# Six-layer float32 block: the start's loads, the companion unit, the index scores and the sparse heads put in another order

## The chip, the core and the metric

The kernel runs on one core of a Trainium2 chip. The metric is the time of the whole execution on the device, in microseconds (us). Engines: PE does matmuls, DVE and POOL elementwise work, ACT activations, SP issues most DMAs. Each engine takes its own queue in order; they meet at semaphores.

## The reference, cut to what matters

Sequence 256, model width 1024, batch 1. Six layers follow each other: a gated short convolution (A0), sparse attention (B0), latent attention (C0), a convolution again (A1), pooling (P0) and stick-breaking attention (S0), each as `x = x + mixer(rmsnorm(x))`. The change is in the first two.

```python
def short_conv_mixer(xn, w_in, conv_w, conv_b, w_out):
    bg, cg, hv, z = jnp.split(xn @ w_in, 4, axis=-1)
    u = cg * hv
    y = causal_depthwise_conv3(u, conv_w) + conv_b
    return (bg * y * jax.nn.silu(z)) @ w_out

def dsa_mixer(xn, positions, w_in, q_norm, k_norm, w_out):
    q, k, v, z, qi, ki, wi = jnp.split(xn @ w_in, cuts, axis=-1)   # 16 heads of 64; 8 index heads
    q = rope(rmsnorm(q, q_norm), positions)
    k = rope(rmsnorm(k, k_norm), positions)
    # qi and ki get a partial rope; per query block of 128:
    rel = jax.nn.relu(jnp.einsum("qhd,sd->qhs", qi_b, ki_b))
    score = jnp.einsum("qh,qhs->qs", w_b, rel)                      # masked by chunks of 64
    top_val, top_idx = lax.top_k(score, 64)
    # per head: softmax over the 64 chosen keys, times v
    return (o * jax.nn.silu(z)) @ w_out
```

## The kernel before

Weights are cut into **units**, 78 in all (A0 begins at 0, B0 at 10, C0 at 22, A1 at 36). A unit's weights land in a slot `raw` of 2 MB, ACT rounds it to `whi` (L409, or L417 in quarters), DVE subtracts to `wlo` (L779, L788), and PE runs three matmuls (xh·whi, xl·whi, xh·wlo) for each pair of tiles, so the product keeps float32's accuracy. There are two slots, so a unit's split runs one or two units ahead of PE. Each engine's order is written out by hand.

**Start.** SP issues the identity, x, the constants `cst`, `a_norm`, then unit 0 in eight pieces, the small parameters, then unit 1. PE transposes x, DVE copies it out and makes xh, xl. Meanwhile POOL works out the rope angles. It waits at its first instruction for the positions and for `cst`:

```python
pool.wait_ge(sem("pos_in"), 48)
pool.wait_ge(sem("cst_in"), 16)
```

and ACT, after the splits of units 0 and 1, waits for POOL's four `angle_ready` steps (L1368 writes the last) before it takes their sines (L496). Only behind that in ACT's queue stand the first unit's copy (L467) and the split of unit 2.

**Layer B** has twelve units. B0 is the index queries; B0+1 (72 columns) is the companion: the index key `ki` and the weights `wi`; B0+2 to B0+6 are q and k by tokens (512 columns); B0+7 k's last part; B0+8 and B0+9 v's rest and z; B0+10, B0+11 the output matrix. Token units are turned to channel-major by PE transposes (`turn_tokens(e)`, e = 0 to 4), after ACT copies them out (`token_raw`), DVE and POOL apply norm and rope (POOL's L1424 the norm factor), and ACT copies the turned result back (`token_out`). With the index queries and key turned, PE does eight index heads, ACT relu (L574), DVE sums them, and DVE picks the top 64 of each query block (`top64`). For each of 16 heads PE then computes scores (2 matmuls), DVE adds the choice and finds the row maximum (L1098, L1102), ACT takes the exponential (L621, L623), DVE divides (L1107, L1109), PE transposes p (L1798), ACT copies it (L630), and PE multiplies with v (PV). Between these, PE has one filler: a quarter of units B0+7, B0+8, B0+9, up to head 11. The silu of z is done on ACT at heads 4 and 12 (L606, with a table load to each side). The output units follow the last head as one block (`out_pair`).

Of the kernel before, what the change touches and what calls it, by code (L numbers as in the profile page):

```python
# [21 lines left out]
F32 = mybir.dt.float32  # L22
# [3 lines left out]
ALU = mybir.AluOpType  # L26
# [84 lines left out]
def build(nc, a, out):  # L111

    ctx = ExitStack()
    with ctx:
# [32 lines left out]
        pl = at("pl", [P, 4, T], F32R, arena_at + 35 * tile_bytes)  # L147
        upad = at("upad", [P, T + 2], F32, arena_at + 18 * tile_bytes)
# [8 lines left out]
        kis = at("kis", [P, NT, P], F32, arena_at + 42 * tile_bytes)  # L157
        ki_b = at("ki_b", [P, NT, 32], F32, arena_at + 43 * tile_bytes)
# [135 lines left out]
        def _(sp):  # L294
# [22 lines left out]
            def conv_layer(u0, j):  # L317

                src = a["a_w_in"][j].rearrange("(k p) (s c) -> s p k c", p=P, s=4)

                def step(b, f, guard):
# [17 lines left out]
                with sp.Fori(1, 4) as i:  # L339
                    for b in range(2):  # L340
                        step(b, i * 2 + b, i * 4 + 2 * (u0 + b) - 2)
# [3 lines left out]
            def small_inputs(first):  # L345

                rows = ((G_A, "a_norm", 16), (G_CW, "a_conv_w", 48), (G_CB, "a_conv_b", 16), (G_B, "b_norm", 8),
                        (G_C, "c_norm", 8), (G_N2, "norm_g_2", 16), (G_NF, "norm_f_2", 8),
                        (G_QL, "c_q_lat_norm", 3), (G_KVL, "c_kv_lat_norm", 2))
                for col, name, c in rows[:1] if first else rows[1:]:  # L350
                    sp.dma_start(grow[col:col + c, 0, :], a[name].rearrange("(n c) -> n c", c=P))\
                        .then_inc(sem("a_norm_in" if first else "grow_in"), 16)
                if first:
                    return
                others = [(grow[G_CQ:G_CQ + 1, 0, 0:96], a["c_q_norm"]), (grow[0:1, 1, 0:96], a["c_k_norm"]),
                           (grow[17:18, 1, 0:64], a["c_k_norm"][:, 0:64]),
                           (grow[1:17, 1, :], a["pool_scale_2"].rearrange("(n c) -> n c", c=P))]
                for dst, src in others:
                    sp.dma_start(dst, src).then_inc(sem("grow_in"), 16)
            sp.dma_start(ident, a["constants"][:, C_ID:C_ID + P]).then_inc(sem("ident_in"), 16)  # L360
            for t in range(NT):
                sp.dma_start(xrow[:, t, :], a["x"][0, t * P:(t + 1) * P, :]).then_inc(sem("x_in"), 16)
            sp.dma_start(cst[:, P:C_COLS], a["constants"][:, P:C_COLS]).then_inc(sem("cst_in"), 16)
            sp.wait_ge(sem("grow_clear"), 1)
            small_inputs(True)
# [38 lines left out]
        def _(act):  # L404
# [3 lines left out]
            def split_half(b, lo, hi):  # L408
                A(whi[b][:, lo:hi], raw[b][:, lo:hi], ACT.Copy).then_inc(hi_ready, 1)  # L409

            def split_quarter(u, q):

                if q == 0:
                    act.wait_ge(landed[u % 2], 64 * (u // 2 + 1))
# [6 lines left out]
            def split(u, part=(0, 1)):  # L421

                cut, end = half_cut(u)
                if 0 in part:
                    act.wait_ge(landed[u % 2], 64 * (u // 2 + 1))
# [6 lines left out]
            def renorm(m, gain):  # L432

                if gain is not None:
                    for n in range(NK):
# [3 lines left out]
                        if m == 0 and n == 3:  # L439
                            act.wait_ge(sem("first_half"), 64)  # L440
                            split_half(0, 0, half_cut(0)[0])
                if m == 0:
# [1593 lines left out]
```

## Time and profile before

| | us |
|---|---|
| median of 3 runs | 1081.18 |
| lowest, highest | 1076.1, 1084.76 |
| profiled execution | 1085.21 |
| its span | 1083.4 |
| PE busy | 1013.5 |
| DVE busy | 649.3 |
| ACT busy | 498.0 |
| POOL busy | 337.4 |

The profiled execution is one of its own; its span is what the profile covers, and 1.81 us of its time lie around the span. PE is busy 94% of the span, so what moves the time is a stretch in which PE waits, or runs at the lower clock, or is given more or less work.

### The profile page before, as it was taken

Reading aid. Unit: us, or ns where it says so; the run is one execution under the profiler, and the core shown is the slowest. Engines: PE = TensorE matmul, PEld = TensorE weight load, DVE = VectorE, ACT = ScalarE, POOL = GpSimd, SP = SyncE. Lnnn points to the kernel's source line nnn. Section 1 sums busy time; section 2 is a strip of 40 time slices with the busy share of each in tenths; the row PEclk is TensorE's granted clock in tenths of the full one; section 3 lists DMA queues with packets and bytes.
Section 4 is the critical chain, followed back from the end, with each engine's and each line's share of the span. In section 5 each row is a group of like instructions: output and inputs, shape, how many; then the busy total and the mean of one; then the engine's idle time right before and its main releaser. Section 6 shows DMA issues by size and latency. Waiting matters only on the chain.

```text
span 1083.4 us, 17563 instructions
## 1 busy us (share of the span) xinstructions
PE 1013.5 (94%) x7165; PEld 935.1 (86%) x7165; DVE 649.3 (60%) x998; ACT 498.0 (46%) x666; POOL 337.4 (31%) x270
## 2 busy tenths in 40 slices
PE   4799999899989989988999999899999999999798
PEld 4799998687759989755899999899999997988698
DVE  3477756895674554458457766677655644555632
ACT  3444345446663434427354336324444336474621
POOL 7944212441110310532143333776400200132400
PEclk8999998899979999759999999999999999999998
DMA  8668445322333313423067754434664462424400
GB/s 230 152 156 232 155 148 175 129 105 78 125 109 103 98 50 97 173 61 79 6 170 184 204 174 172 160 122 164 218 235 158 169 214 92 155 79 155 156 1 39
DMA packets 127526, 148.49 MB, mean 137 GB/s; under 512 B 12595, under 2 KB 83520, under 8 KB 127456
## 3 DMA queue, kind: packets, MB, share of 16 engines
q1 hardware_dynamic: 127008, 146.39, 42.1%
q0 software_dynamic: 448, 1.12, 0.4%
q8 instruction: 50, 0.82, 0.3%
q14 instruction: 20, 0.16, 0.0%
HBM read 146.44 MB, written 1.05 MB: 136 GB/s over the span
## 4 chain that ended last, share of the span: by engine, by line
PE 62%; DVE 8%; ACT 5%; POOL 3%; issue 3%; DVEq 0%; ACTq 0%; POOLq 0%
PE acc L1501 38%; PE aux L1501 23%; POOL arena L1374 1%; DVE wlo L779 1%; POOL arena L1375 1%; POOL arena L1373 1%; PE aux L1798 1%; ACT whi L417 1%; ACT arena L447 1%; DVE wlo L788 1%; DVE score L1056 1%; DVE work L1098 1%; DVE top L1055 1%; DVE sqy L989 0%; DVE arena L871 0%
## 5 line engine op out<-in xcount | busy, mean ns | idle before, releaser
L779 DVE TENSOR_TENSOR wlo<-raw,whi 128x2048 fp32r<-128x2048 f32 (+4 forms) x132 | 295.2, 2264 | 145.4 <-ACT whi L409 143.6
L1501 PE MATMUL acc<-xh,whi 128*128 128x256 f32 (+1 forms) x1200 | 346.0, 288 | 12.3 <-DVE wlo L779 10.1
L1501 PE MATMUL acc<-xl,whi 128*128 128x256 f32 (+1 forms) x1200 | 342.8, 286 | 0.0
L1501 PE MATMUL acc<-xh,wlo 128*128 128x256 f32 (+1 forms) x1200 | 342.7, 286 | 0.0
L409 ACT ACTIVATE whi<-raw 128x2048 fp32r<-128x2048 f32 (+4 forms) x132 | 215.1, 1661 | 118.1 <-PE aux L1501 66.5
L1501 PEld LDWEIGHTS acc<-xh,whi 128*128 128x128 f32 (+1 forms) x1200 | 233.3, 194 | 16.5 <-DVE wlo L779 10.4
L1501 PEld LDWEIGHTS acc<-xl,whi 128*128 128x128 f32 (+1 forms) x1200 | 233.6, 195 | 0.0
L1501 PEld LDWEIGHTS acc<-xh,wlo 128*128 128x128 f32 (+1 forms) x1200 | 233.4, 194 | 0.0
L1501 PE MATMUL aux<-yh,whi 128*128 128x256 f32 x384 | 108.9, 284 | 0.0
L1501 PE MATMUL aux<-yh,wlo 128*128 128x256 f32 x384 | 108.7, 283 | 0.0
L1501 PE MATMUL aux<-yl,whi 128*128 128x256 f32 x384 | 108.7, 283 | 0.0
L1445 POOL CAST yh<-ytmp 128x256 fp32r<-128x256 f32 x24 | 19.7, 822 | 232.5 <-DVE ytmp L1293 129.3
L1501 PE MATMUL acc<-whi,xh 128*128 128x512 f32 (+1 forms) x192 | 76.6, 399 | 3.6 <-DVE arena L871 1.5
L1501 PE MATMUL acc<-wlo,xh 128*128 128x512 f32 (+1 forms) x192 | 74.9, 390 | 0.0
L1501 PE MATMUL acc<-whi,xl 128*128 128x512 f32 (+1 forms) x192 | 74.8, 390 | 0.0
L1501 PEld LDWEIGHTS aux<-yh,whi 128*128 128x128 f32 x384 | 73.7, 192 | 0.3 <-issue 0.3
L1501 PEld LDWEIGHTS aux<-yl,whi 128*128 128x128 f32 x384 | 73.7, 192 | 0.0
L1501 PEld LDWEIGHTS aux<-yh,wlo 128*128 128x128 f32 x384 | 73.7, 192 | 0.0
L788 DVE TENSOR_TENSOR wlo<-raw,whi 128x1024 fp32r<-128x1024 f32 x48 | 58.4, 1218 | 0.4 <-ACT whi L417 0.3
L1501 PE MATMUL aux<-arena 64*128 64x128 f32 (+2 forms) x224 | 55.2, 382 | 2.5 <-ACT relu L574 1.6
L1373 POOL TENSOR_TENSOR arena<-arena 128x1024 f32<-128x1024 f32 x5 | 12.0, 2409 | 137.5 <-ACT arena L447 137.5
L417 ACT ACTIVATE whi<-raw 128x1024 fp32r<-128x1024 f32 x48 | 50.1, 1045 | 0.0
(283 smaller groups left out, 1724.8 us busy)
## 6 DMA issues: line engine op xcount, KB each, us to landing
raw<-in_a_w_in SPq DMA_DIRECT2D x60, 512.0 KB, 6.5
raw<-in_sb_w_in SPq DMA_DIRECT2D x48, 512.0 KB, 5.7
raw<-in_b_w_in SPq DMA_DIRECT2D x36, 512.0 KB, 5.2
raw<-in_pool_w_in SPq DMA_DIRECT2D x32, 512.0 KB, 5.8
raw<-in_a_w_out SPq DMA_DIRECT2D x16, 512.0 KB, 4.8
raw<-in_pool_w_out SPq DMA_DIRECT2D x16, 512.0 KB, 4.9
raw<-in_sb_w_out SPq DMA_DIRECT2D x16, 512.0 KB, 5.2
raw<-in_c_w_in SPq DMA_DIRECT2D x12, 512.0 KB, 5.4
```

The costliest lines, as they stand in the source:

```text
L409: A(whi[b][:, lo:hi], raw[b][:, lo:hi], ACT.Copy).then_inc(hi_ready, 1)
L417: ins = A(whi[u % 2][:, c * q:c * q + c], raw[u % 2][:, c * q:c * q + c], ACT.Copy)
L447: A(arena[:, 4 * n:4 * n + 4, :], xT[:, 4 * n:4 * n + 4, :], ACT.Square)\
L779: TT(wlo[b][:, lo:hi], raw[b][:, lo:hi], whi[b][:, lo:hi].bitcast(F32), ALU.subtract)\
L788: ins = TT(wlo[u % 2][:, c], raw[u % 2][:, c], whi[u % 2][:, c].bitcast(F32), ALU.subtract)
L1055: me.link(V.max(top8[:, :], s))
L1056: me.link(V.match_replace(s, top8[:, :], s, TAKEN))
L1098: ins = V.tensor_tensor_reduce(L[:, lo:hi], S[:, lo:hi], bias[:, lo:hi], -1.0, 3.0e38, ALU.add, ALU.min, st[:, n:n + 1])
L1373: me.link(TT(arena[:, 0:4, :], arena[:, 0:4, :], arena[:, 4:8, :], ALU.add))
L1374: me.link(TT(arena[:, 0:2, :], arena[:, 0:2, :], arena[:, 2:4, :], ALU.add))
L1445: nc.gpsimd.tensor_copy(hi, ytmp[:, :]).then_inc(sem("yh_ready"), 1)
L1501: return nc.tensor.matmul(out_, lhsT, rhs, start=start, stop=stop, skip_group_check=True)
```

## The change

Four things are changed.

1. **Loads at the start.** x comes in column halves. Unit 0's and unit 1's weights come in eight pieces by rows of the matrix. The constants are issued behind unit 0's eight pieces. Unit 2 has a buffer of its own (`raw_third`). The 13 small parameters go by ACT's queue. Units 0 and 1 are split in quarters, and layer A0's sum of squares goes ahead of unit 1's split on DVE.
2. **Companion.** B0+1 is computed channel-major (72 rows by 256), 24 matmuls in place of 48; ACT copies it to `kif`, and two transposes inside unit B0+2 give its token rows.
3. **Index scores.** One index head stands before each of the eight steps of unit B0+4, q's unit, in place of all eight behind B0+3. The turns of tokens are moved into the units (k = 2, 4 or 6), and the splits of B0+5 into the loop of relus.
4. **Sparse heads by pairs.** Both heads' scores are issued together, with two fillers for each pair, the pair's transposes one pair later, and its two PVs together behind the second filler. Half of output unit B0+10 is done as fillers 13 to 16; the other half and B0+11 follow.

```diff
                 if u0 == 0:
-                    dst = slot(0, 8, 512)
-                    for k, signal in ((0, sem("first_half")), (4, landed[0])):
-                        for s in range(4):
-                            sp.dma_start(dst[:, k:k + 4, s * P:s * P + P], src[s][:, k:k + 4, 0:P]).then_inc(signal, 16)
-                    small_inputs(False)
-                    step(1, 1, None)
+                    for k in range(8):
+                        first_tile(0, k).then_inc(sem(f"first_in{k // 2}"), 16)
+                    sp.dma_start(cst[:, P:C_COLS], a["constants"][:, P:C_COLS]).then_inc(sem("cst_in"), 16)
+                    for k in range(8):
+                        first_tile(1, k).then_inc(sem(f"second_in{k // 2}"), 16)
+                    whole(raw_third, 2, landed[0])
+                    step(1, 3, 4)
...
-            token_unit(B0 + 1, spread_at(1, 6))
+            unit(B0 + 1, [(acc[0:72, 2, 0:T], 0, 72)], xh, xl)
...
             taken("tok_raw", 2)
-            token_unit(B0 + 2)
...
+            token_unit(B0 + 2, ki_rows)
             taken("ki_raw", 2)
-            token_unit(B0 + 3)
-            taken("ki_out", 1)
-            taken("tok_out", 2)
-            for h in range(8):
...
+            token_unit(B0 + 3, ki_turn)
             taken("tok_raw", 4)
-            token_unit(B0 + 4)
-            turn_tokens(2)
+            token_unit(B0 + 4, index_scores)
             taken("tok_raw", 6)
-            token_unit(B0 + 5)
-            turn_tokens(3)
+            token_unit(B0 + 5, turn_at({2: 1}))
             taken("tok_raw", 8)
-            token_unit(B0 + 6)
+            token_unit(B0 + 6, turn_at({2: 2, 6: 3}))
...
+            def sparse_heads(q, k, v):
+
+                for j in range(HEADS // 2 + 1):
+                    if j < HEADS // 2:
+                        if j:
+                            pe.wait_ge(sem("logits"), 2 * j)
...
+                        for c, e in ((0, P), (P, T)):
+                            for i in (2 * j, 2 * j + 1):
...
+                    sparse_filler(2 * j)
+                    if j == 0:
+                        taken("v_ready", 2)
+                        turn_tokens(4)
+                    if j:
+                        for h in (2 * j - 2, 2 * j - 1):
+                            pe.wait_ge(sem("p_ready"), h + 1)
...
+                            ins.then_inc(sem("pt_psum"), 1)
+                    sparse_filler(2 * j + 1)
+                    if j:
+                        t = j - 1
+                        pe.wait_ge(sem("pt_ready"), 2 * t + 2)
+                        if t:
+                            pe.wait_ge(sem("y_ready"), 8 + t)
...
-            softmax_heads(0, pair(0), pair(8), vB)
-            out_pair(B0 + 10, 8)
+            sparse_heads(pair(0), pair(8), vB)
+            sparse_last_out()
```

POOL's program is the same in both kernels, and so are ACT's and DVE's loops over the 16 heads.

SP's queue from its first DMA, before (`raw_49` is unit 0's slot):

```order
L360 DMA cst<-in_constants 128x128
L362 DMA xrow<-in_x 128x1024 x2
L363 DMA cst<-in_constants 128x623
L351 DMA grow<-in_a_norm 16x128
L333 DMA raw_49<-in_a_w_in 128x4x128 x8
L351 DMA grow<-in_a_conv_w 48x128
L351 DMA grow<-in_a_conv_b 16x128
L351 DMA grow<-in_b_norm 8x128
```

and after the change:

```order
L360 DMA cst<-in_constants 128x128
L364 DMA xrow<-in_x 128x512 x4
L327 DMA raw_49<-in_a_w_in 128x4x128 x8
L346 DMA cst<-in_constants 128x623
L327 DMA raw_50<-in_a_w_in 128x4x128 x8
L333 DMA raw_third<-in_a_w_in 128x8x128 x4
L340 DMA raw_50<-in_a_w_in 128x8x128 x4
```

The constants (128x623) moved from the third place to behind unit 0's eight pieces, and the small parameters (`grow`) left this queue.

PE at the end of unit B0+3 and the first index scores, before (`aux<-arena` are the scores, `acc<-` the weights' matmuls):

```order
L1501 MATMUL acc<-whi_52,xh 128x512
L1501 MATMUL acc<-wlo_54,xh 128x512
L1501 MATMUL acc<-whi_52,xl 128x512
L1501 MATMUL aux<-arena 128x128
L1501 MATMUL aux<-arena 128x256
```

and after, the end of B0+3 and the first step of B0+4:

```order
L1549 MATMUL acc<-whi_52,xl 128x512
L1549 MATMUL aux<-arena 128x128
L1549 MATMUL aux<-arena 128x256
L1549 MATMUL acc<-whi_51,xh 128x512
L1549 MATMUL acc<-wlo_53,xh 128x512
L1549 MATMUL acc<-whi_51,xl 128x512
```

Before, seven more such pairs of scores follow at once; now six matmuls of 512 columns stand behind each pair (the first three are shown), and the next pair behind them.

PE within the heads, before, from the last filler matmuls of one head to the next head's (`aux<-cst,work` are the transposes of p, `acc<-work,vB` is PV, `aux<-arena` are scores):

```order
L1501 MATMUL acc<-xh,wlo_54 128x256
L1798 MATMUL aux<-cst,work 128x128 x3
L1501 MATMUL acc<-work,vB 64x256
L1501 MATMUL acc<-work,vB 64x128
L1501 MATMUL aux<-arena 128x128
L1501 MATMUL aux<-arena 128x256
L1501 MATMUL acc<-whi_51,xh 128x512
```

and after, at the same place:

```order
L1549 MATMUL acc<-xh,wlo_54 128x256
L1549 MATMUL acc<-work,vB 64x256 x2
L1549 MATMUL acc<-work,vB 64x128 x2
L1549 MATMUL aux<-arena 128x128 x2
L1549 MATMUL aux<-arena 128x256 x2
L1549 MATMUL acc<-whi_51,xh 128x512
```

PV and scores of two heads stand together; the six transposes of a pair stand between its two fillers, ahead of this piece.

## Rows read from the trace of the kernel before

**Rows 1.** The page: busy us, share of the span and instructions of each engine.

```profile
PE 1013.5 (94%) x7165; PEld 935.1 (86%) x7165; DVE 649.3 (60%) x998; ACT 498.0 (46%) x666; POOL 337.4 (31%) x270
```

**Rows 2.** The timeline of SP's queue: start, length of the issue in us.

```profile
2.13 0.43 SPq L363 DMA_DIRECT2D cst<-in_constants  x1
```

**Rows 3.** Tile views in that stretch: landing of `cst` (two transfers), then of `raw`'s first eight.

```profile
DMA to landing us min/median/max: 1.9/4.7/7.5
L333 SPq DMA_DIRECT2D raw<-in_a_w_in x8: 825/862/3312, 3.5 to 12.4; - x8
DMA to landing us min/median/max: 5.3/7.8/8.1
```

**Rows 4.** Timeline of POOL's angle chain, and the DVE split beside it.

```profile
9.91 0.40 POOL L1351 CAST arena<-table 128x256 f32<-128x256 int32 x1 [5.27 <-DMA pos_i<-in_positions]
...
22.42 2.15 POOL L1364 TENSOR_TENSOR work<-work,ang 128x96 f32<-128x96 f32 x1
25.19 0.39 POOL L1364 TENSOR_TENSOR work<-work,ang 128x96 f32<-128x96 f32 x1
...
22.03 2.29 DVE L779 TENSOR_TENSOR wlo<-raw,whi 128x2048 fp32r<-128x2048 f32 x1 [1.16 <-ACT whi L409]
...
48.87 1.07 POOL L1368 TENSOR_SCALAR work<-work 128x256 f32<-128x256 f32 x1
```

**Rows 5.** Timeline behind it, on ACT, DVE and PE: unit 2's first half.

```profile
49.97 0.72 ACT L496 ACTIVATE table<-work 128x256 f32<-128x256 f32 x2 [9.17 <-POOL work L1368]
...
50.86 1.91 ACT L409 ACTIVATE whi<-raw 128x2048 fp32r<-128x2048 f32 x1
...
55.15 0.39 PE L1501 MATMUL acc<-xh,whi 128*128 128x256 f32 x1 [3.08 <-DVE wlo L779]
```

**Rows 6.** Windows: busy us (instructions) on each engine, granted clock, DMA share, GB/s.

```profile
60.00:140.00 80.00, 80.00 (x669) 80.00 (x668) 56.18 (x66) 35.45 (x38) 28.35 (x22) 1.00 0.64 188
220.00:230.00 10.00, 10.00 (x50) 8.28 (x49) 9.86 (x15) 2.91 (x4) 7.50 (x4) 1.00 0.21 60
```

**Rows 7.** PE's timeline, the first index scores (four records for a head).

```profile
192.71 0.93 PE L1501 MATMUL aux<-arena 64*128 64x128 f32 x8
```

**Rows 8.** PE's timeline over one head of the sparse softmax.

```profile
267.07 0.86 PE L1501 MATMUL acc<-work,vB 128*64 128x256 f32 x4
267.86 0.92 PE L1501 MATMUL aux<-arena 64*128 64x128 f32 x4
268.71 0.50 PE L1501 MATMUL acc<-whi,xh 128*128 128x512 f32 x1
...
271.59 0.49 PE L1798 MATMUL aux<-cst,work 128*128 128x128 f32 x3
```

**Rows 9.** PE's timeline, first row of unit B0+1 and of B0+2.

```profile
160.15 0.28 PE L1501 MATMUL acc<-whi,xh 128*128 128x72 f32 x1
...
167.80 0.77 PE L1501 MATMUL acc<-whi,xh 128*128 128x512 f32 x1 [0.61 <-DVE wlo L779]
```

**Rows 10.** Timeline on DVE, POOL and PE where the heads begin.

```profile
245.51 0.28 DVE L1098 CUSTOM_DVE_ANT_0 work<-aux,pick 128x128 f32<-128x128 f32 x1
...
249.48 1.17 POOL L1424 TENSOR_TENSOR sqy<-sqy,hf 128x512 f32<-128x512 f32 x1
...
251.59 0.63 PE L1656 MATMUL acc<-cst,sqy 128*128 128x128 f32 x4 [2.36 <-ACT arena L544]
```

**Rows 11.** Timeline over head 12: ACT's silu between its table loads, and PE.

```profile
309.25 1.28 ACT L606 ACT_TABLE_LOAD   x1
310.54 1.06 ACT L606 ACTIVATE arena<-arena 128x1024 f32<-128x1024 f32 x1
...
312.25 1.08 PE L1501 MATMUL acc<-work,vB 128*64 128x256 f32 x2 [3.81 <-DVE ytmp L1078]
```

**Rows 12.** Windows over the heads, columns as in Rows 6.

```profile
252.00:310.00 58.00, 54.50 (x319) 42.58 (x316) 32.95 (x107) 34.54 (x73) 4.55 (x8) 0.97 0.20 73
310.00:320.00 10.00, 7.75 (x23) 4.37 (x23) 7.04 (x25) 7.85 (x15) 2.25 (x4) 0.58 0.38 122
```

More of the change, by code:

```diff
@@ L338, in conv_layer @@
                         step(b, b, 2 * (u0 + b) - 2)
-                with sp.Fori(1, 4) as i:
+                with sp.Fori(2 if u0 == 0 else 1, 4) as i:
                     for b in range(2):
@@ L343, in conv_layer @@
                     plain(u0 + 8 + h, a["a_w_out"][j], 4 * h, 0)
[L345 to L359, printed above, removed]
-            sp.dma_start(ident, a["constants"][:, C_ID:C_ID + P]).then_inc(sem("ident_in"), 16)
[L361 to L365, printed above, removed]
+            sp.dma_start(ident, a["constants"][:, C_ID:C_ID + P]).then_inc(sem("ident_in"), 16)
+            for half in range(2):
+                c = slice(512 * half, 512 * half + 512)
+                for t in range(NT):
+                    sp.dma_start(xrow[:, t, c], a["x"][0, t * P:(t + 1) * P, c]).then_inc(sem(f"x_in{half}"), 16)
             conv_layer(A0, 0)
@@ L424, in split @@
                 if 0 in part:
[L425 removed]
+                    act.wait_ge(landed[u % 2], 64 * (u // 2))
                     if u >= 2:
@@ L487, in _ @@
             renorm(0, G_A)
-            split(1)
+            for q in range(4):
+                first_quarter(1, q)
             root(0)
@@ L828, in renorm @@
                                 .then_inc(sem("xg_ready"), 1)
-                    if m == 0 and c in (2, 4):
-                        split(0, (c // 4,))
+                    if m == 0 and c:
+                        first_quarter(0, c - 1)
             def token_squares(m):
@@ L880, in _ @@
             renorm(0, G_A)
-            split(1)
             token_squares(0)
+            for q in range(4):
+                first_quarter(1, q)
             dve.wait_ge(sem("g_psum"), 1)
@@ L924, in _ @@
             split(B0 + 1)
-            factor(1)
+            factor(1, spread=False)
             split(B0 + 2, (0,))
@@ L1766, in v_unit, with sparse_filler @@
                     ins.then_inc(unit_done, 1)
+            def sparse_filler(f):
+                part = (2 * (f % 4), 2)
+                if f == 0:
+                    taken("tok_raw", 10)
+                if f == 4:
+                    taken("z_raw", 1)
+                if f == 8:
+                    taken("v_ready", 4)
+                if f < 12:
+                    if f // 4 == 1:
+                        v_unit(B0 + 8, 1, *part)
+                    else:
+                        unit(B0 + 7 + f // 4, in_tiles(1), xh, xl, part=part)
+                if 13 <= f < 17:
+                    if f == 13:
+                        taken("z_raw", 2)
+                    sparse_out(f - 13, 0)
@@ new lines, in sparse_out @@
+            def sparse_out(k, half):
+                wh, wl = w_view(B0 + 10, 4, 1024)
+                if k % 2 == 0:
+                    pe.wait_ge(lo_ready, 2 * (B0 + 10) + 1 + k // 2)
+                pe.wait_ge(sem("yl_ready"), 8 + k + 1)
+                for n in range(4):
+                    c = slice(512 * half + P * n, 512 * half + P * n + P)
+                    ins = three(sparse_out_tile(4 * half + n), wh[:, k, c], wl[:, k, c], yh[:, k, :], yl[:, k, :],
+                                k == 0 and n % 2 == 0)
+                if k == 3 and half == 1:
+                    ins.then_inc(unit_done, 1)
@@ new lines, in sparse_last_out @@
+            def sparse_last_out():
+                for k in range(4):
+                    sparse_out(k, 1)
+                u = B0 + 11
+                wh, wl = w_view(u, 4, 1024)
+                pe.wait_ge(lo_ready, 2 * u + 2)
+                pe.wait_ge(sem("yl_ready"), 16)
+                for n in range(NK):
+                    c = slice(P * n, P * n + P)
+                    for k in range(4):
+                        ins = three(sparse_out_tile(n), wh[:, k, c], wl[:, k, c], yh[:, 4 + k, :], yl[:, 4 + k, :], False)
+                    if n % 2 and n < NK - 1:
+                        ins.then_inc(sem("out_bank"), 1)
+                ins.then_inc(unit_done, 1)
```

233 lines of the change are left out of this document (156 added, 77 removed).

## The prediction

> **What bounds the kernel now.** First the page's totals: PE is busy 1013.5 of 1083.4 us, so all that can be gained is the 70 us in which it waits, its time at half clock, and its own work [rows 1]. Then the windows: from 60 to 140 PE is busy 80.00 of 80 at a granted clock of 1.00, so what the start gains or loses ahead of 60 reaches the end whole [rows 6]. In layer B the window 220 to 230 shows DVE at 9.86 of 10, with PE full as well [rows 6]. The timelines then tell which wait ends last at the two places that the change touches: unit 2's first matmul at 55.15, and the stretch from the heads' start to C0.
>
> **The start.** Unit 2 begins at 55.15, behind DVE's `wlo`, behind ACT's split at 50.86, behind the sines at 49.97, for which ACT had stood idle 9.17 us on POOL [rows 5]. POOL's chain runs without a break from 9.91 to 49.94 [rows 4]. So here neither the weights nor the splits set PE's restart, but the time at which POOL begins; POOL's program is unchanged and waits for `cst`. Quarters, row pieces and `raw_third` gain nothing behind it: they only let units 0 and 1 finish earlier, and PE waits longer for unit 2.
>
> What the change moves is `cst`. Before, it is issued at 2.13 [rows 2] and lands 7.5 later (the longer of its two landings), at 9.6 [rows 3]. Now it stands behind the eight pieces; the last of those was issued at 12.4 and took 5.3 at the least, so it landed at 17.7 [rows 3]. The bytes ahead in the queue are the same, with `cst` last in place of third, so I let it land at 17.7: POOL begins 8.1 later. One of the eight issues took 3.3 in place of 0.86 [rows 3]; if that stall goes, it is 5.7. Against it, POOL's operations lengthen beside DVE's splits: 2.15 where the same one takes 0.39 alone, 1.8 more, while the split at 22.03 ran [rows 4]. Five or so fall into the chain before; with POOL later and DVE's work earlier I take one fewer, between none and three: 1.8 back. Sum: 8.1 - 1.8 = **+6.3**, between +1 (5.7 - 5.4 is 0.3) and +8.
>
> The Trainium skill (SBUF — State Buffer, Terms) has an exclusive lock on a port pair that DVE and GpSimd share, by which the loser "fully blocks"; the lengthened row agrees. By that rule alone the number of splits beside the chain counts and not their size, and quarters would make the lengthened operations twice as many and half as long; the sum would stay.
>
> **Layer B up to the heads.** PE's saving is plain. B0+1 begins at 160.15 and B0+2 at 167.80 [rows 9]: 7.65 for 48 matmuls at half clock, a spread and a wait; 24 matmuls of 256 columns take the 2.9 of a filler (12 matmuls of 512 columns or 24 of 256) [rows 8]. Taken out of its single file, index scores lose their overlap: two heads took 0.93 together [rows 7], and a single head takes 0.92 by the head's row [rows 8], so eight now take 7.4 in place of 3.7, while the waits on relu between them go. Turns inside units are the same work. In all PE could reach its first head some 6 us earlier. But the first softmax row on DVE is at 245.51, where PE has been waiting: its next matmul, the last turn, starts at 251.59 behind POOL's factor at 249.48 (1.17 long), which follows DVE [rows 10]. DVE is full [rows 6], and its list up to there has the same operations; only waits at its head go. I take 1.2 of the 6 us, between 0 and 2: **-1.2**.
>
> **The heads.** From 251.6 on, five terms.
> - Filler 1. Before, it ran ahead of the turn, while PE had to wait anyway; now it stands behind the turn. Its cover is gone: from 268.71 to 271.59, **+2.9** [rows 8].
> - Scores. One head takes 0.85 (267.86 to 268.71) [rows 8]; two heads on the two halves of the array's rows took 0.93 [rows 7]. Fourteen heads singly are 11.9, seven pairs 6.5: **-5.4**.
> - PV. One head takes 0.79 (267.07 to 267.86) [rows 8]. Two heads write the two halves of PSUM's partitions, each using half of the array's columns. No row shows two of these together. Bounds: no overlap, 16 × 0.79 = 12.6 as before; full overlap as the scores, 8 × 0.86 = 6.9. The nearest row is the index pair, which overlaps fully, so I take **-5.7**, with 0 as the other end.
> - Waits. ACT's silu at heads 4 and 12 costs its queue 1.28 + 1.06 + 1.28 = 3.6 [rows 11]. Before, it cost PE nothing at head 4 and 3.81 at head 12 [rows 11]; all of PE's waits come to 3.50 from 252 to 310 and 2.25 from 310 to 320, 5.8 in all [rows 12]. By pairs, PV of heads 2 and 3 needs ACT's copy of head 3, which stands behind head 5's exponential, behind the silu. Counted from pair 4/5's scores, with durations of the same operations in neighbouring heads: scores 0.9, DVE's copy of z 1.3, maximum 0.8, exponential 1.1, copy 0.5, quarter split 1.0, silu 3.6, exponential 1.1, copy 0.5: 10.8. PE has for that time the scores 0.9, two fillers 2 × 2.9 and six transposes 0.7: 7.4. PE waits 3.4. At head 12 the z copy is early, 9.5, but PE's fillers are none and 12 matmuls (1.45): 3.1, so 6.4. Behind it two short ones of 1.9 and 0.8, for the same lack of filler. Together 12.5 in place of 5.8: **+6.7**.
> - Clock. From 310 to 320, around its long wait, PE is granted 0.58, near the lower level of 1.2 GHz, where 252 to 310 shows 0.97 [rows 12]; that tail stays. The new wait at head 4 has the length of that one and should bring PE down once more. The price is between 0 and 2.9 (one filler at half the speed takes twice its 2.9 [rows 8]); I take the middle, **+1.5**.
>
> The output's half unit is moved and is the same work: it fills waits that would else be 5.8 longer, and is counted there. Sum of layer B: -1.2 + 2.9 - 5.4 - 5.7 + 6.7 + 1.5 = **-1.2**.
>
> On PV the Trainium skill (TensorE: Matmul & The Clock Gate, Part 3: Packing small matmuls — row/col tiling) speaks both ways: its table gives three column tiles 2.38 times the speed of one after the other, yet it lets a weight load overlap a running matmul "only when row_grp differs", which it doesn't in PV. By the table the sum stays near its value; by the second rule PV gains nothing, rival A below.
>
> **Sum.** 6.3 - 1.2 = +5.1 on an execution of 1085.2, which is 1090.3. That execution lies 4.0 above the median of 1081.18, and the comparison is by medians: **1086.3**, within 1%.
>
> **Rivals.**
> - A. PV pairs don't overlap: +5.7, of which about a third falls into waits behind the silus, +3.9 net; 1090.2. If the scores don't overlap either (+5.4, again a part in waits, +4.1), 1094.3. Slower than before by 1.2%, decided by whether two heads' records take more than 1.6 us together. For it: PV's weights use all 128 rows, and the scores' interleaving differs from the index heads'. Against: [rows 7].
> - B. `cst` isn't late, or POOL's chain isn't what unit 2 waits for: the start costs 0. Layer B as summed: 1080.0. For it: the landing at 17.7 is of a queue whose order within 16 engines I can't see. Against: ACT's 9.17 us on POOL [rows 5].
> - C. Faster: DVE doesn't hold the heads back, because its orders move too (splits of B0+5 inside the index loop), so 6 us come through in place of 1.2, and the silu waits are half as long (-3.4). 4.8 and 3.4 off the forecast's 1086.3 are 1078.1; without the late `cst` 1071.8. For it: PE does reach its heads earlier; against: DVE's 9.86 of 10 [rows 6].
> - D. Unit 2's weights come too late: they stand behind `cst` and unit 1's eight pieces, whose issue is 8 × 0.86 = 6.9 [rows 3]. Issued at 21 and landed 8 later they are there at 29, ACT asks for them at 57; it costs nothing unless the queue stalls for 28 us, so it is a mishap without a price.
>
> **How the numbers follow.** The forecast's case has 0.40; A 0.27 (0.17 with scores overlapping, 0.10 without); B 0.15; C 0.15, a quarter of it without the late `cst`; D 0.03. A measurement of this kernel can hardly tell 1% (10.8 us) from no change. The range leaves out C's end and the worst of A with waits longer still: 1074 to 1096. Slower by over 1% (over 1092): most of A's second part, and part of its first and of the forecast's case if the waits are longer, 0.28. Faster by over 1% (under 1070.4): the far end of C and what I haven't seen, 0.16. Within: 0.56.
>
> **What would show it.** The profile after should have POOL's first angle operation at about 18 in place of 10, its last near 56, unit 2's first matmul near 61, and units 0 and 1 done by 42. B0+1 should take 3 us. The turn should start at 256 to 257 (250.4 by the time of before, and the start's 6), with PE idle 10 us ahead of it in two or three pieces. In the heads, records of two heads' scores should span 0.9 and of two PVs 0.9 or 1.6, with a wait of 3 to 4 us before the PV of heads 2 and 3, and one of 5 to 6 before that of heads 10 and 11, released by ACT's copy. It is wrong if unit 2 starts before 58, if the turn starts more than 3 us earlier than before beyond the start's shift, or if PE's waits in the heads sum to under 8 us.

## The result and the profile after

The changed kernel takes 1086.22 us (median of 16 runs, 1082.92 to 1088.37), the kernel before 1080.13 (16 runs, 1075.43 to 1085.39). The ratio is 1.0045, 95% interval 1.0026 to 1.0065: 4.9 us slower (2.8 to 7.0), within 1%. The two medians themselves are 6.1 apart. The profiled execution of after took 1082.92, the lowest of its sixteen, and its span is 1081.1, shorter than the 1083.4 of before's; so the two spans can't be set against each other as a whole, and this document compares stages.

The page's totals of after, to be read beside [rows 1]:

```profile
PE 987.7 (91%) x7143; PEld 915.5 (85%) x7143; DVE 649.0 (60%) x1002; ACT 498.5 (46%) x671; POOL 332.9 (31%) x270
```

PE is busy 26 us less. Little of that is gain: the span is only 2.3 shorter, so PE stands idle 93 us in place of 70, longer at the start and ahead of the turn, and overlapping matmuls count once.

The start: SP's timeline, then how long `cst`'s two transfers took to land (minimum, median, maximum), then the chain POOL, ACT, PE. These answer to [rows 2 to 5].

```profile
3.10 10.11 SPq L327 DMA_DIRECT2D raw<-in_a_w_in  x8
13.24 0.82 SPq L346 DMA_DIRECT2D cst<-in_constants  x1
```

```profile
DMA to landing us min/median/max: 1.9/3.7/5.4
```

```profile
18.81 1.21 POOL L1399 CAST arena<-table 128x256 f32<-128x256 int32 x1 [14.18 <-DMA cst<-in_constants]
...
55.56 1.07 POOL L1416 TENSOR_SCALAR work<-work 128x256 f32<-128x256 f32 x1
...
56.66 0.72 ACT L519 ACTIVATE table<-work 128x256 f32<-128x256 f32 x2 [18.90 <-POOL work L1416]
57.56 1.90 ACT L434 ACTIVATE whi<-raw_third 128x2048 fp32r<-128x2048 f32 x1
...
61.83 0.58 PE L1549 MATMUL acc<-xh,whi 128*128 128x256 f32 x1 [21.15 <-DVE wlo L807]
```

The constants are issued at 13.24 and land 5.4 later, at 18.6; POOL's first operation waits 14.18 us and begins at 18.81 in place of 9.91. Its chain takes 37.8 us (to 56.63) where it took 40.0. The sines follow at 56.66, unit 2's split at 57.56, and unit 2 starts at 61.83 where it started at 55.15: 6.7 later. PE stood idle 21.15 us ahead of it.

PE around the companion and at the last turn of tokens (see [rows 9, 10]):

```profile
166.97 0.32 PE L1549 MATMUL acc<-xh,whi 128*72 128x256 f32 x1
173.23 0.47 PE L1549 MATMUL acc<-whi,xh 128*128 128x512 f32 x1 [3.25 <-DVE wlo L807]
...
252.56 1.08 PE L1712 MATMUL acc<-cst,sqy 128*128 128x128 f32 x4 [5.04 <-POOL sqy L1472]
257.26 1.09 PE L1712 MATMUL acc<-cst,sqy 128*128 128x128 f32 x4 [3.62 <-ACT arena L567]
```

B0+1 takes 3 us in place of 7, but B0+2 waits 3.25 for its split. The last turn is done in two pieces, with 5.04 and 3.62 idle ahead of them; 2.44 stand ahead of filler 0.

PE in the heads (see [rows 8, 11]):

```profile
269.40 0.87 PE L1549 MATMUL acc<-work,vB 128*64 128x256 f32 x8
270.20 0.93 PE L1549 MATMUL aux<-arena 64*128 64x128 f32 x8
...
281.69 1.55 PE L1549 MATMUL acc<-work,vB 128*64 128x256 f32 x8 [4.20 <-ACT work L658]
...
312.53 0.55 PE L1905 MATMUL aux<-cst,work 128*128 128x128 f32 x3 [1.11 <-DVE work L1157]
...
320.13 1.55 PE L1549 MATMUL acc<-work,vB 128*64 128x256 f32 x8 [5.63 <-ACT work L658]
...
329.20 0.87 PE L1549 MATMUL acc<-work,vB 128*64 128x256 f32 x8 [1.47 <-ACT work L658]
332.99 0.87 PE L1549 MATMUL acc<-work,vB 128*64 128x256 f32 x8 [0.63 <-ACT work L658]
```

Two heads' PVs take 0.80 (269.40 to 270.20) and their scores 0.86 (to the filler at 271.06): full overlap in both. The waits are 4.20 ahead of the PV of heads 2 and 3, 1.11 + 5.63 at head 12, and 1.47 and 0.63 behind it.

The windows of the last heads, columns as in [rows 6] (see [rows 12]), and the start of C0 (before: 349.18):

```profile
310.00:320.00 10.00, 3.39 (x28) 2.60 (x26) 6.32 (x21) 7.58 (x15) 1.12 (x2) 0.90 0.00 0
320.00:326.00 6.00, 5.87 (x33) 4.51 (x34) 2.92 (x11) 2.19 (x6) 0.00 (x0) 0.59 0.78 265
326.00:333.00 7.00, 4.90 (x43) 4.14 (x41) 6.60 (x16) 4.80 (x10) 2.39 (x3) 1.00 0.20 72
```

```profile
351.15 0.28 PE L1549 MATMUL acc<-xh,whi 128*128 128x256 f32 x1
```

From 310 to 320 the granted clock is 0.90 where before showed 0.58; PE is idle for 6.6 of these 10 us. Behind the wait it falls to 0.59 for 6 us and is back at 1.00 from 326.

**By stages.** Every run left one profile. Its landmarks on PE are B0's first matmul, the second piece of the last turn (before: the row at 251.59), C0's first matmul, and the end of the span. All values in us.

| kernel | start to B0 | B0 to turn | turn to C0 | C0 to end |
|---|---|---|---|---|
| before | 148.88 | 102.71 | 97.59 | 734.2 |
| before, again | 149.09 | 102.65 | 95.20 | 727.7 |
| before, constants late | 157.57 | 102.85 | 96.71 | 729.9 |
| before, silu first | 148.28 | 102.67 | 93.08 | 733.4 |
| after | 155.69 | 101.57 | 93.89 | 730.0 |
| after, again | 156.32 | 104.21 | 94.88 | 730.8 |
| constants early | 150.88 | 103.20 | 94.91 | 730.5 |
| filler first | 155.55 | 101.55 | 92.69 | 736.8 |
| heads in turn | 156.32 | 101.61 | 94.15 | 733.4 |
| silu first | 156.00 | 103.13 | 84.77 | 727.7 |
| no half unit | 155.92 | 101.57 | 102.39 | 734.1 |
| early, sines later | 149.58 | 103.17 | 94.55 | 733.5 |
| index together | 156.14 | 108.06 | 94.35 | 733.6 |
| all four | 148.73 | 103.12 | 83.71 | 733.4 |

Means over the kernels that share a stage word for word: the start 155.99 (7 with the changed loads) against 148.75 (3): **+7.2**. Layer B's front 102.57 (9 of the changed order, without "index together") against 102.72 (4): **-0.15**. Heads and output 94.52 (5) against 96.50 (3): **-2.0**, known to about one us, since the three profiles of before spread from 95.20 to 97.59. Sum +5.1, and 4.9 was measured. The last column holds the same 5,154 PE instructions in all of them and spreads from 727.7 to 736.8 for kernels of both kinds. PE's busy time in it goes along, from 694.0 to 701.9: most of the spread is the same matmuls taking longer.

### The profile page after: what moved, and what is told of

Its sections match the earlier page's. It is cut to its first block, busy times and chain, and to the rows that moved or that the text cites. A ratio compares the mean times of both kernels' runs of the same rounds, so it can differ in the third digit from the quotient of the medians.

```text
span 1081.1 us, 17522 instructions
## 1 busy us (share of the span) xinstructions
PE 987.7 (91%) x7143; PEld 915.5 (85%) x7143; DVE 649.0 (60%) x1002; ACT 498.5 (46%) x671; POOL 332.9 (31%) x270
## 4 chain that ended last, share of the span: by engine, by line
PE 61%; DVE 8%; ACT 5%; POOL 3%; issue 3%; DVEq 0%; ACTq 0%; POOLq 0%
PE acc L1549 38%; PE aux L1549 21%; POOL arena L1422 1%; POOL arena L1423 1%; POOL arena L1421 1%; ACT whi L442 1%; DVE wlo L826 1%; DVE work L1146 1%; DVE wlo L807 1%; ACT arena L468 1%; DVE score L1104 1%; DVE top L1103 1%; DVE stat L1150 1%; ACT work L651 0%; ACT vS L627 0%
## 5 line engine op out<-in xcount | busy, mean ns | idle before, releaser
L807 DVE TENSOR_TENSOR wlo<-raw,whi 128x2048 fp32r<-128x2048 f32 (+5 forms) x126 | 282.0, 2265 | 132.5 <-ACT whi L434 130.5
L434 ACT ACTIVATE whi<-raw 128x2048 fp32r<-128x2048 f32 (+5 forms) x126 | 203.8, 1649 | 107.4 <-PE aux L1549 60.4
L1549 PE MATMUL aux<-yh,whi 128*128 128x256 f32 x352 | 99.9, 284 | 0.0
L1549 PE MATMUL aux<-yh,wlo 128*128 128x256 f32 x352 | 99.6, 283 | 0.0
L1549 PE MATMUL aux<-yl,whi 128*128 128x256 f32 x352 | 99.6, 283 | 0.0
L1549 PE MATMUL acc<-whi,xh 128*128 128x512 f32 x176 | 71.8, 408 | 5.3 <-DVE wlo L807 3.2
L1549 PE MATMUL acc<-whi,xl 128*128 128x512 f32 x176 | 69.2, 393 | 0.0
L1549 PE MATMUL acc<-wlo,xh 128*128 128x512 f32 x176 | 69.1, 393 | 0.0
L1549 PEld LDWEIGHTS aux<-yh,whi 128*128 128x128 f32 x352 | 67.6, 192 | 0.3 <-issue 0.3
L1549 PE MATMUL aux<-arena 64*128 64x256 f32 (+2 forms) x224 | 49.1, 387 | 0.9 <-DVE arena L988 0.9
```

Of the source, the lines that this page charges most:

```text
L434: A(whi[b][:, lo:hi], (raw_third if third else raw[b])[:, lo:hi], ACT.Copy).then_inc(hi_ready, 1)
L807: TT(wlo[b][:, lo:hi], (raw_third if third else raw[b])[:, lo:hi], whi[b][:, lo:hi].bitcast(F32), ALU.subtract).then_inc(lo_ready, 1)
L1549: return nc.tensor.matmul(out_, lhsT, rhs, start=start, stop=stop, skip_group_check=True)
```

## The experiments

Each ratio is to the kernel before executed beside that run. Its median was 1080.13 beside after and 1081.88 to 1083.86 beside the runs below, so kernels are best compared by their ratios; after's is 1.0045.

**The start, from both sides.** First the changed kernel with the constants early.

```diff
-                    sp.dma_start(cst[:, P:C_COLS], a["constants"][:, P:C_COLS]).then_inc(sem("cst_in"), 16)
...
+            sp.dma_start(cst[:, P:C_COLS], a["constants"][:, P:C_COLS]).then_inc(sem("cst_in"), 16)
             conv_layer(A0, 0)
```

> The changed kernel with the constants issued right behind x again, as before, and nothing else. Theory 1 (POOL's angle chain sets unit 2): POOL starts near 10, unit 2's first matmul is back at 55 +- 1 in place of 61.8, the time falls by 6 to 7 us against the changed kernel, to about 1079.5, a ratio to before of 0.999 or less (layer B's gain in the profile was 4.8). Rival (unit 2 waits for its own weights or the moved small parameters): unit 2 stays beyond 59 and the time above 1084.

```profile
12.12 0.40 POOL L1399 CAST arena<-table 128x256 f32<-128x256 int32 x1 [7.47 <-DMA cst<-in_constants]
...
57.10 0.58 PE L1549 MATMUL acc<-xh,whi 128*128 128x256 f32 x1 [14.73 <-DVE wlo L807]
```

Measured: 1080.74 us (12 runs), ratio to before 0.9977 (0.9954 to 1.0000): 5.5 less than after by the times, 7 by the ratios, 5.1 by the start's column. POOL starts at 12.12 and not at 9.91: the constants are issued at 3.10 behind x's four pieces (before 2.13) and take 8.9 to land (before 7.5). Unit 2 starts at 57.10, 1.1 above the 55 +- 1 expected. The theory holds, with 2 us of the delay left in place.

Then the kernel before with the constants late.

```diff
-            sp.dma_start(cst[:, P:C_COLS], a["constants"][:, P:C_COLS]).then_inc(sem("cst_in"), 16)
...
+                    sp.dma_start(cst[:, P:C_COLS], a["constants"][:, P:C_COLS]).then_inc(sem("cst_in"), 16)
                     small_inputs(False)
                     step(1, 1, None)
```

> The kernel before with one edit: the constants are issued behind unit 0's eight pieces. Theory 1: POOL's first operation at 18 to 19, unit 2's first matmul at 61 to 62 in place of 55.15, the time 6 to 7 us longer than before (ratio 1.006). Rival (the cost came from quarters and row pieces, not from the constants): the time as before, within 2 us.

```profile
18.87 0.40 POOL L1351 CAST arena<-table 128x256 f32<-128x256 int32 x1 [14.23 <-DMA cst<-in_constants]
...
63.23 0.58 PE L1501 MATMUL acc<-xh,whi 128*128 128x256 f32 x1 [10.06 <-DVE wlo L779]
```

Measured: 1091.02 us (9 runs), ratio 1.0066 (1.0032 to 1.0101). POOL at 18.87, unit 2 at 63.23, 8.1 later than before and 1.2 beyond what was expected; B0 starts 8.7 later. One DMA's place in SP's queue makes the whole loss of the start, alone, in the old kernel. In the changed kernel B0 is 1.6 earlier than here (155.99 against 157.57); which of quarters, row pieces, third buffer and moved parameters brings that wasn't separated.

**Filler 1 ahead of the last turn.**

```diff
                     sparse_filler(2 * j)
-                    if j == 0:
-                        taken("v_ready", 2)
-                        turn_tokens(4)
...
                     sparse_filler(2 * j + 1)
+                    if j == 0:
+                        taken("v_ready", 2)
+                        turn_tokens(4)
```

> The changed kernel with the last turn of tokens put behind filler 1, where it stood before. Theory 1: filler 1 runs while PE waits for POOL and DVE, so the time from the turn to C0 shortens by filler 1 and its half-clock part, 3 to 4 us; C0 starts 3 to 4 us earlier than in the changed kernel (351.15). Rival (DVE and ACT set the heads' pace from there, so that PE waits at head 4 for longer): under 1 us.

PE behind the last turn:

```profile
257.10 1.09 PE L1712 MATMUL acc<-cst,sqy 128*128 128x128 f32 x4 [4.07 <-ACT arena L567]
258.12 1.65 PE L1549 MATMUL aux<-arena 64*128 64x128 f32 x8
```

Measured: C0 at 349.79, 1.4 earlier; 1086.85 us (10 runs), ratio 1.0031 (0.9999 to 1.0064), no difference from after that these runs can tell. The filler did go under the wait, but the half-clock stretch behind the turn now lies on the scores (1.65 in place of 0.93) and on the next filler, 4.6 long in place of 3.1, of which after had lost 1.0 in filler 1. Neither the theory's 3 to 4 nor the rival's under 1.

**The two heads one behind the other.**

```diff
-                        for c, e in ((0, P), (P, T)):
-                            for i in (2 * j, 2 * j + 1):
+                        for i in (2 * j, 2 * j + 1):
+                            for c, e in ((0, P), (P, T)):
...
-                        for n in range(2):
-                            for h in (2 * t, 2 * t + 1):
+                        for h in (2 * t, 2 * t + 1):
+                            for n in range(2):
```

> The changed kernel with the two heads of a pair one behind the other, scores and PV both, and everything else of the pair order kept. Theory 1 (the halves of the array overlap only where two heads' matmuls stand interleaved): scores of a pair take 1.7 and PVs 1.6 in place of 0.93 and 0.87, C0 starts 7 to 11 us later. Rival (the overlap needs no interleaving, as the index heads of the kernel before showed it): a pair takes the same 0.9 and C0 starts within 1 us.

The PVs of heads 0 and 1, and the scores of heads 4 and 5:

```profile
270.19 0.88 PE L1549 MATMUL acc<-work,vB 128*64 128x256 f32 x8
271.00 0.93 PE L1549 MATMUL aux<-arena 64*128 64x128 f32 x8
```

Measured: the rows are as in after (0.81 from the first PV to the scores), and turn to C0 takes 94.15 against 93.89; 1088.24 us (10 runs), ratio 1.0034 (1.0008 to 1.0061). The rival is right: two heads on different halves of the array overlap when they are neighbours in the queue; interleaving their matmuls adds nothing.

**The silu ahead of the exponentials.**

```diff
+                    if layer == 0 and i in (4, 12):
+                        silu(24 if i == 4 else 28, 4, 1 if i == 4 else 2)
+                        nc.scalar.preload_act_table_set("natural_log_exp_and_others")
                     if i < HEADS:
                         L, st = logit_buf(i)
...
-                    if layer == 0 and i in (4, 12):
-                        silu(24 if i == 4 else 28, 4, 1 if i == 4 else 2)
-                        nc.scalar.preload_act_table_set("natural_log_exp_and_others")
```

> The changed kernel with ACT's silu of z (and its two table loads) ahead of the exponentials of heads 4 and 12 in place of behind them. Theory 1 (the silu stands between PE's transposes and the copy of head 3 or 11, and so makes the waits of 4.2 and 5.6 before PV): most of one table load and the silu run while ACT is idle anyway, the two waits shrink to under 2.5 and 4, C0 starts 3 to 5 us earlier. Rival (the exponentials, now behind the silu, delay the same chain by as much): C0 within 1 us.

ACT around the silu, and PE at the two places of the long waits:

```profile
272.81 1.28 ACT L634 ACT_TABLE_LOAD   x1
274.10 1.06 ACT L634 ACTIVATE arena<-arena 128x1024 f32<-128x1024 f32 x1
275.18 1.28 ACT L648 ACT_TABLE_LOAD   x1
276.48 0.49 ACT L652 ACTIVATE work<-work,stat,nf 128x128 f32<-128x128 f32 x1
...
280.46 0.76 PE L1549 MATMUL acc<-work,vB 128*64 128x256 f32 x6 [0.32 <-ACT work L661]
...
313.77 0.44 PE L1549 MATMUL acc<-work,vB 128*64 128x256 f32 x2 [3.10 <-ACT work L661]
```

Measured: the waits are 0.32 in place of 4.20 and 3.10 in place of 5.63; turn to C0 takes 84.77 in place of 94.52. Of these 9.8, 6.4 are the two waits, and most of the rest is clock: behind the 0.32 at head 4 PE's matmuls keep their full speed, where PV and scores behind the 4.20 took 1.55 and 1.65. 1075.46 us (10 runs), ratio 0.9951 (0.9922 to 0.9980): faster than the kernel before by 0.5%. The cause of the two waits is shown; the expected 3 to 5 was too small.

The same edit in the kernel before:

> The kernel before with ACT's silu ahead of the exponentials of heads 4 and 12. Theory 1 (the silu's place is a fault of both orders, not of the pairs): the wait of 3.81 at head 12 and the half-clock tail behind it shrink, C0 starts 2 to 6 us earlier than 349.2. Rival (only the pair order waits on copies behind the silu): C0 within 1 us.

Measured: turn to C0 93.08 against 96.50 (its wait at head 12 is 2.51 in place of 3.81); 1078.09 us (10 runs), ratio 0.9965 (0.9939 to 0.9990). PE's wait of 0.90 at head 4 (before: at 274.62, on a DVE split behind ACT's silu) is gone as well. The place of the silu costs both orders, the pair order about three times as much.

**Without the half unit in the heads.**

```diff
-                if 13 <= f < 17:
-                    if f == 13:
-                        taken("z_raw", 2)
-                    sparse_out(f - 13, 0)
...
-                for k in range(4):
-                    sparse_out(k, 1)
+                taken("z_raw", 2)
+                for half in range(2):
+                    for k in range(4):
+                        sparse_out(k, half)
```

> The changed kernel with fillers 13 to 16 taken out of the heads; the first half of output unit B0+10 is done behind the last head, as the rest. Theory 1 (the half unit fills waits of the last heads, and holds the clock up): its 48 matmuls, 5.8 us, appear behind the heads, the heads themselves end less than 2 us earlier, and the granted clock of the last 12 us of heads falls towards 0.6: C0 starts 5 to 9 us later. Rival (the fillers delay the transposes and PVs that they stand ahead of): C0 starts 2 us later or less.

PE's waits at heads 12 and 14, and the windows of the last heads and of the output:

```profile
320.67 1.55 PE L1549 MATMUL acc<-work,vB 128*64 128x256 f32 x8 [7.05 <-ACT work L658]
329.70 1.55 PE L1549 MATMUL acc<-work,vB 128*64 128x256 f32 x8 [3.42 <-ACT work L658]
```

```profile
320.00:334.00 14.00, 8.58 (x40) 5.12 (x42) 10.03 (x26) 7.52 (x18) 2.79 (x4) 0.50 0.43 150
334.00:360.00 26.00, 26.00 (x200) 25.48 (x198) 8.47 (x10) 6.34 (x8) 1.51 (x3) 0.90 0.33 107
```

Measured: turn to C0 takes 102.39, 7.9 more; 1095.89 us (4 runs), ratio 1.0134 (1.0082 to 1.0185). The last PV is at 333.31 and was at 332.99: taking 5.8 us of matmuls out of the heads ends them no earlier. From 320 to 334 the granted clock is 0.50 (after: 0.82), and it is not back at full when the output begins (0.90 from 334 to 360): 2.1 us on top of the 5.8. Nor is all of the 5.8 waits. PE's waits from the turn to C0 sum to 17.42 us here and to 13.36 in after, 4.1 more; the rest of the 7.9 is the lower clock.

**The index heads together again.**

```diff
-                if h == 0:
-                    taken("ki_out", 1)
-                    taken("tok_out", 2)
-                if h >= 2:
-                    pe.wait_ge(sem("idx_relu"), h - 1)
+                if h:
+                    return
+                taken("ki_out", 1)
+                taken("tok_out", 2)
+                for h in range(8):
+                    if h >= 2:
+                        pe.wait_ge(sem("idx_relu"), h - 1)
```

> The changed kernel with all eight index heads ahead of unit B0+4's first matmul, as before the change, and the rest kept. Theory 1 (DVE holds layer B's front, so PE's order there hardly reaches the heads): the last turn's end and C0 move by less than 1.5 us. Rival (single index heads inside q's unit are what brings layer B's front forward): the last turn starts 3 us or more later.

PE's two long waits, and ACT's relu ahead of the second:

```profile
202.95 3.92 PE L1549 MATMUL aux<-arena 64*128 64x128 f32 x12 [2.35 <-ACT relu L601]
209.76 0.58 PE L1549 MATMUL aux<-arena 64*128 64x128 f32 x1 [2.90 <-ACT relu L601]
```

```profile
209.22 0.49 ACT L601 ACTIVATE relu<-aux 128x384 f32<-128x384 f32 x1 [4.05 <-DVE score L1081]
```

Measured: B0 to turn takes 108.06 in place of 102.57; 1093.06 us (4 runs), ratio 1.0077 (1.0054 to 1.0101). Theory 1 falls. With the splits of B0+5 inside DVE's and ACT's loops over the index heads, as the change has them, PE would stand 2.35 and 2.90 ahead of single relus that wait for DVE, which is splitting; B0+4 begins 13 us later (211.33 against 197.90) than with the heads in the unit, and DVE, done with the first top 64 at 223.4, then stands idle for 7.83. PE's order does reach the turn where it makes DVE wait. (The kernel before has the heads together and the splits outside; its front takes 102.72.)

**Constants early and the sines behind unit 2's split.** ACT's waits for `angle_ready` and its sines stand behind unit 2's second split, and DVE splits that half before it waits for POOL.

```diff
-            act.wait_ge(sem("angle_ready"), 2)
...
                     split_half(b, SLOT // 2, SLOT, third)
+                    if third:
+                        act.wait_ge(sem("angle_ready"), 2)
...
+                    if third:
+                        dve.wait_ge(hi_ready, u * 2 + 6)
+                        split_half(b, SLOT // 2, SLOT, third)
                     dve.wait_ge(sem("u_ready"), j + (8 * k + 1))
```

> The changed kernel with the constants early and with ACT's sines moved from ahead of unit 2's split to behind it (DVE splits unit 2's second half before it waits for POOL). Theory 1 (only the sines' place in ACT's queue ties unit 2 to POOL's angle chain): unit 2 starts at 43 to 45 in place of 57.1, PE then waits at unit 3 instead, which starts at 61 to 65 in place of 69; the start gains 4 to 8 us on the kernel with the constants early. Rival (unit 2's weights, behind unit 1's, aren't there): unit 2 not before 50.

The end of POOL's chain, DVE's convolution that waits for it, and PE at unit 3:

```profile
53.16 1.07 POOL L1421 TENSOR_SCALAR work<-work 128x256 f32<-128x256 f32 x1
...
59.03 0.79 DVE L952 TENSOR_SCALAR arena<-upad,G 128x256 f32<-128x256 f32 x1 [15.46 <-POOL upad L1392]
...
66.22 0.58 PE L1554 MATMUL acc<-xh,whi 128*128 128x256 f32 x1 [12.29 <-DVE wlo L808]
```

Measured: unit 2 follows unit 1 without a wait, but unit 3 starts at 66.22 behind 12.29 of idle time, and B0 at 149.58, 1.3 earlier than with the constants early alone. 1081.01 us (10 runs), ratio 0.9989 (0.9960 to 1.0018). The 4 to 8 us expected didn't come. POOL's chain ends at 54.23, DVE's first convolution waits for POOL's `upad` behind it until 59.03, and unit 3's split stands behind that. The wait moved by one unit. The edit also lengthened the chain: it took 43.3 us from 10.90, where it took 39.8 from 12.12 with the constants early alone. DVE now splits unit 2 from 38.50 to 43.57, and beside it two of POOL's operations take 2.21 and 2.77, where operations of the same two kinds take 0.7 and 0.9 alone.

**All four edits together** (constants early, sines later, filler first, silu first).

> The changed kernel with the constants early, the sines later, filler 1 ahead of the last turn, and the silu first. Theory 1: the gains add up, 4.7 from the constants, 4 to 8 from the sines, 1.2 from the filler, 3 to 5 from the silu: 12 to 18 us under the changed kernel's 1086.2, so 1068 to 1074, clear of the kernel before by 0.7% or more. Rival (what is gained ahead of layer C is given back by the granted clock in C): not under 1078.

Measured: 1066.12 us (6 runs, 1064.63 to 1072.22), ratio 0.9863 (0.9820 to 0.9905), 20 under after, where 12 to 18 were expected, and 1.4% faster than the kernel before. The single edits sum to 5.1 (start, constants) + 1.3 + 1.8 + 9.8 = 18.0 by the stages' columns; this kernel's own columns against the means of the changed order: -7.3, +0.55, -10.8, which is 17.5. The profiled execution was 4.7 above the median, so the last 2 us of the 20 can't be placed. The rival, that layer C gives it back (not under 1078), fell by the time itself; C0 to end is 733.4, within the other kernels' spread.

**The same programs again.**

> The kernel before, unchanged. Theory (the granted clock in layer C, and with it the time from C0 to the end, differs between executions of one program): C0 starts at 349 +- 1 as in the first profile, but the rest takes something else than 734.2 us, by 2 to 7. Rival (each program has its own clock pattern): the rest is 734 within 1.

> The changed kernel, unchanged. Theory: C0 starts at 351 +- 1 and the rest takes something else than 730.0 us, nearer to 734 since the median is 3.3 above the first profiled execution. Rival: 730 within 1.

The windows over layer C of the kernel before, first and second execution, columns as in [rows 6]:

```profile
420.00:460.00 40.00, 38.30 (x240) 32.77 (x239) 17.46 (x22) 18.52 (x22) 15.08 (x9) 0.83 0.43 143
460.00:500.00 40.00, 33.73 (x133) 23.19 (x132) 25.69 (x87) 16.80 (x44) 12.89 (x11) 0.66 0.18 45
```

```profile
420.00:460.00 40.00, 39.63 (x251) 34.21 (x250) 22.80 (x27) 17.62 (x20) 19.74 (x12) 0.85 0.49 160
460.00:500.00 40.00, 32.54 (x136) 21.76 (x135) 27.67 (x105) 19.94 (x55) 10.52 (x11) 0.73 0.12 32
```

Measured: C0 to end 727.7 in place of 734.2 for the kernel before, so the first theory holds there; 730.8 in place of 730.0 for after, where it doesn't. C0's own start was expected to repeat within 1 us and did in neither: 346.94 in place of 349.18, and 355.41 in place of 351.15. The second execution of before has PE busy 39.63 + 32.54 with granted clocks 0.85 and 0.73, the first 38.30 + 33.73 with 0.83 and 0.66. After's two differ in layer B instead, B0 to turn 104.21 and 101.57. The window behind the wait of 3.25 ahead of B0+2 shows why, the first execution first:

```profile
168.00:178.00 10.00, 6.75 (x40) 5.79 (x39) 6.79 (x9) 7.77 (x7) 1.26 (x2) 1.00 0.34 112
```

```profile
168.00:178.00 10.00, 6.75 (x33) 5.66 (x32) 6.50 (x11) 8.37 (x8) 0.72 (x1) 0.73 0.37 133
```

Same idle time (PE busy 6.75 in both), clock 1.00 and 0.73. In the nine profiles of this order the window around the wait has 1.00 four times, and B0 to turn is 101.6; 0.83 or 0.84 four times, and it is 103.1 to 103.2; 0.73 once, and it is 104.2. What decides between them isn't known.

## Why the prediction was right, point by point

The time was forecast at 1086.3 and is 1086.22; the difference at +5.1 and is 4.9. The sum is nearer than its terms, and that is luck: the start and the front came out 2 us worse than forecast and the heads 2 us better. The match of the times is luck too. The forecast stood on a median of 1081.18 from three runs of before, the sixteen beside after gave 1080.13, and the two medians are 6.1 apart. Rivals A, B and C are out by the rows: PV pairs overlap, the start lost 7.2, and neither did the 6 us come through nor were the waits halved.

- **The start, +6.3; measured +7.2.** The mechanism is right in every row: POOL at 18.8, its last angle at 55.56, unit 2 at 61.83. The constants landed 9.0 later and not 8.1. The credit for less sharing with DVE was 1.8 and is 2.2 (chain 37.8 in place of 40.0), so the delay at unit 2 is 6.7; another half us is lost by B0. By its own figures the forecast's lower bound was +0.3 and not +1.
- **The front, -1.2; measured -1.1 in the first profile, -0.15 on the mean.** B0+1's saving and the waits came as said (2.44 + 5.04 + 3.62 = 11.1 idle ahead of the turn). It left out that the new wait of 3.25 ahead of B0+2 costs a half-clock stretch in five of nine executions. B0+1's 7.65 us before weren't all at half clock either: from 160.15 to 164.60 the granted clock is 1.00, and only the last 2.6 us show 0.54; the saving is the same. The reason given for the -1.2 was too simple as well: the step "only waits at its head go" took DVE as bound whatever PE does, and "index together" lost 5.5 us by PE's order alone.
- **Filler 1, +2.9; measured 1.8 on the mean** (94.52 - 92.69). The cover was gone as said; part of the price went into the clock term.
- **Scores -5.4 and PV -5.7; measured -5.9 and -6.2.** Both overlap fully: 0.93 for two heads as forecast, and 0.80 for two PVs where one took 0.79. The forecast set the length of a pair's record (0.93, 0.86) against a single head's time from start to start; from start to start the pairs take 0.86 and 0.80, so seven are 6.0 against 11.9 and eight 6.4 against 12.6. The Trainium skill's table on packing (TensorE: Matmul & The Clock Gate, Part 3: Packing small matmuls — row/col tiling) gives three column tiles 2.38 times the speed of one after the other; the two PVs agree, with 1.98 times. Taken as a bar on PV, its sentence that weight loads overlap "only when row_grp differs" would have made two PVs 1.6.
- **Waits +6.7; measured** 4.20 + 0.32 + 1.11 + 5.63 + 1.47 + 0.63 = 13.4 against 5.8: **+7.6**. The chain through the silu was 10.8 by hand for head 4 and the wait 3.4; it was 4.2. "Silu first" shows the cause. That the silu "cost PE nothing at head 4" before was misread: the wait of 0.90 there goes away with it.
- **Clock +1.5; about +0.7 is left for it. The step that failed inside the right sum.** The new stretch at half clock behind the wait at head 4 came as said (PV 1.55 in place of 0.87). "That tail stays" failed: before, the clock is 0.58 from 310 to 320 and 0.56 to 326; after, it is low only from 320 to 326, 0.59. The row of before from 320, then after's row over the 14 us of "no half unit":

```profile
320.00:326.00 6.00, 6.00 (x23) 3.49 (x22) 5.25 (x11) 3.36 (x8) 1.56 (x2) 0.56 0.38 147
```

```profile
320.00:334.00 14.00, 11.77 (x81) 9.34 (x82) 9.53 (x26) 7.00 (x16) 3.19 (x4) 0.82 0.45 152
```

The half output unit keeps PE busy in the last heads: without it the clock is 0.50 over these 14 us. The forecast counted the half unit for 5.8 us of waits filled and nothing else; it fills 4.1 of waits, and 3.8 more are clock. The tail of before isn't a constant either: executed again, its clock from 310 to 326 is 0.68 in place of 0.57. The heads as a whole were forecast at 0.0 (the front's -1.2 apart) and came to -2.0; with the terms above as measured, 1.8 - 5.9 - 6.2 + 7.6 = -2.7, and +0.7 is left where +1.5 stood, with the uncertainty of the -2.0.

## What to carry to other kernels

Before moving a small transfer behind large ones, ask which engine's first instruction waits for it, and what chain hangs on that; here 0.3 MB of constants cost 7 us. When two items of work are paired so that a longer round trip stands between their waits, look for the one-off operations (a table load, a silu) inside that round trip and put them where their engine idles: here this took 9.8 us off, where the heads' new order as a whole had brought 2.0. Work that fills waits is worth the waits and also the clock that it holds up.

## What the runs showed of the hardware that wasn't expected

- Two matmuls with 128 rows and 64 columns each, to different halves of PSUM's partitions, overlap in full: two heads' PVs in 0.80 where one took 0.79. They need not be interleaved, only be neighbours.
- One program's granted clock differs between executions behind the same wait: 1.00 and 0.73 in the ten us around the 3.25 us wait at 173; and the stretch from C0 to the end took 727.7 to 736.8 us over fourteen profiles with the same instructions. That is more than the whole change, and why single profiled executions mislead here: after's span was 2.3 shorter than before's.
- POOL's operations beside DVE's quarter splits are lengthened often and a little (1.1 to 1.5 in place of 0.4), beside halves seldom and much (2.15 in place of 0.39). The chain as a whole took 39.8 with quarters and the constants early, and 40.0 in the kernel before.
